# A diffusion block's input projection, done in two sweeps with high and low parts of its weight

## The reference

```python
cq, ckv, kr, rq, rk, rv, rg = jnp.split(h @ w_in, IN_SPLITS, axis=-1)   # widths 256,128,32,512,512,512,512
q_a, k_a, v_a = mla_qkv(cq, ckv, kr, ...)                 # latent attention: norm, w_uq, w_ukv, rope
o_att = block_attention(q_a, [k_a, k_ac], [v_a, v_ac])
q_r, k_r, v_r = retention_qkv(rq, rk, rv, row, col)       # rope; 8 heads of 64
# per chunk of 128 tokens, forwards and backwards in time:
s = einsum(qc, kc) * decay_in;  y_inner = einsum(s, vc);  y_cross = einsum(qc * xi, r_prev)
r = decay_chunk * r + einsum(kc * zeta, vc)               # the carried state
y_ret = norm(y_fwd + y_bwd) * g_ret * silu(rg)
x = x + ga1 * (concat([o_att, y_ret]) @ w_o)              # then the expert layer
```

## Time and profile before

| | us |
|---|---|
| median of 3 runs (lowest, highest) | 3234.02 (3233.12, 3239.76) |
| the profiled execution, its own time | 3241.32 |
| span of its trace, first to last instruction | 3239.5 |
| first product with `w_in` starts | 145.5 |
| last record of the projection starts (L525) | 889.5 |
| retention: first instruction, last one | 897.8, 1103.6 |
| first product of the attention | 1120.0 |

### The profile page before, as it was taken

How to read it: one execution, slowest core, us unless ns; L and a number is a source line. 1 busy time by engine, 2 the same in 40 slices (tenths; PEclk the granted TensorE clock), 3 DMA queues, 4 the chain that set the end, 5 groups by cost and what they waited for, 6 DMA issues and landing times. The chain is left out here.

```text
span 3239.5 us, 55402 instructions
## 1 busy us (share of the span) xinstructions
PE 2990.5 (92%) x20325; PEld 2205.0 (68%) x20325; DVE 2014.4 (62%) x2973; ACT 1381.0 (43%) x2069; POOL 353.2 (11%) x385
## 2 busy tenths in 40 slices
PE   6799999999978699999999998899399999999997
PEld 1355555555578667666666665787398989899996
DVE  1133333333357599989899998445766666666766
ACT  0133333333222377677677765211244444444444
POOL 0011111111145200000000000221001111010102
PEclk9899999999977699999999999999599999999998
DMA  8511111111132301110111000533467676666768
GB/s 313 176 65 64 64 60 61 61 64 64 52 111 78 82 3 34 37 25 14 35 27 25 23 6 12 179 135 113 137 205 209 206 222 208 201 203 211 212 202 312
DMA packets 255042, 365.51 MB, mean 113 GB/s; under 512 B 36469, under 2 KB 170616, under 8 KB 253177
## 3 DMA queue, kind: packets, MB, share of 16 engines
q1 hardware_dynamic: 245336, 327.97, 31.5%
q0 software_dynamic: 9504, 34.61, 4.5%
HBM read 280.70 MB, written 81.83 MB: 112 GB/s over the span
## 5 line engine op out<-in xcount | busy, mean ns | idle before, releaser
L479 PE MATMUL bank<-w_in_sb,h_T 128*128 128x512 f32 (+1 forms) x1440 | 609.9, 578 | 2.1 <-DVE h_T L628 2.1
L1784 PE MATMUL ebank<-gathered_T,w_gate_up 128*128 128x256 f32 x4608 | 561.2, 284 | 21.8 <-issue 16.4
L1784 PEld LDWEIGHTS ebank<-gathered_T,w_gate_up 128*128 128x128 f32 x4608 | 556.7, 193 | 25.6 <-issue 20.7
L479 PEld LDWEIGHTS bank<-w_in_sb,h_T 128*128 128x128 f32 x1440 | 270.4, 191 | 299.4 <-issue 299.1
L1062 PE MATMUL abank<-head_qT,head_kT 96*128 96x512 f32 x1728 | 414.7, 400 | 23.2 <-DVE head_qT L1171 17.0
L1062 PEld LDWEIGHTS abank<-head_qT,head_kT 96*128 96x128 f32 x1728 | 326.3, 192 | 104.6 <-issue 29.6
L1142 ACT ACTIVATE scores<-scores 128x1536 f32<-128x1536 f32 x192 | 274.3, 1476 | 232.8 <-DVE scores L1201 232.8
L1201 DVE TENSOR_TENSOR scores<-scores,abank 128x1536 f32<-128x1536 f32 x192 | 322.7, 1748 | 44.9 <-PE abank L1082 44.8
L1137 ACT ACTIVATE scores<-abank 128x512 f32<-128x512 f32 x576 | 325.7, 602 | 42.5 <-PE abank L1062 17.1
L1092 PE MATMUL abank<-scores,head_v 128*64 128x256 f32 x2304 | 291.0, 388 | 1.2 <-ACT scores L1142 1.2
L1798 PE MATMUL ebank<-w_down,hidden_T 128*128 128x512 f32 x1152 | 282.0, 400 | 2.9 <-DVE w_down L2016 2.8
(11 more groups left out here) (266 smaller groups left out, 3291.8 us busy)
## 6 DMA issues: line engine op xcount, KB each, us to landing
w_gate_up_whole<-in_w_exp_gate SPq DMA_DIRECT2D x48, 1024.0 KB, 5.7
w_gate_up_whole<-in_w_exp_up SPq DMA_DIRECT2D x48, 1024.0 KB, 9.0
w_down_whole<-in_w_exp_down SPq DMA_DIRECT2D x192, 256.0 KB, 6.0
ada_w<-in_w_ada SPq DMA_DIRECT2D x12, 2048.0 KB
scratch_ret<-ret_rows SPq DMA_DIRECT2D x72, 256.0 KB, 2.5
x_tile<-in_x_all SPq DMA_DIRECT2D x18, 512.0 KB
w_in_sb<-in_w_in SPq DMA_DIRECT2D x4, 2048.0 KB, 18.2
chunk_qk<-scratch_ret SPq DMA_DIRECT2D x16, 512.0 KB
```

The lines of the kernel that those rows point to most:

```text
L479: m = pe.matmul(banks[bank][:, 0:n], hT[u][:, k, :], w_in[:, k, lo:lo + n], start=(k == 0), stop=(k == KD - 1))
L1784: x = pe.matmul(banks[f % 3][:, j * CAP:(j + 1) * CAP], w_gu[c][:, wp, j, k, o:o + P], xsT[:, xp, k, :], start=(k == 0 and n == 0), stop=( ...
```

## The change

`w_in` and h are split into high and low parts, and each product is three `fp32r` matmuls. The columns are divided over two sweeps.

**Going up** (`project`, 18 turns): latents, retention keys and values only, 24 matmuls each. h is written to memory (`scratch_h`, 512 KB a tile) before its low part overwrites it, and the chunk's state goes to memory too. Attention queries are made for the 16 latent tiles only. The three weight parts needed here are split during `modulation`, on ACT and DVE. The query and gate columns (4 MB) are loaded at the start of `project` and only used in the next stage.

**Going down** (`retention`, 16 turns): h, keys, values and states are read back; each turn forms the queries and gates of the next chunk (`z_query`, `z_gate`, 24 matmuls each), ropes the query, takes the gate, and does the retention of its own chunk, in this order on each engine. Query and gate weights are split at its start, 16 pieces of 128x512. The scaled-query and score tiles have one buffer instead of two, and scores no longer run ahead.

The core of the diff:

```diff
+
+def modulation(nc, ins, perm, scratch, weights, w_loaded, w_rest):
 
     with stage_semaphores(nc) as sem, ExitStack() as ctx:
...
+            for part, c in enumerate(IN_PARTS):
+                act.wait_ge(w_loaded[1 + part], 16)
+                act.activation(weights["in"][:, 0, :, c], weights["in_whole"][:, 1, :, c], ACT.Copy).then_inc(s_w_in, 1)
...
+                if 5 <= n < 8:
+                    c = IN_PARTS[n - 5]
+                    dve.wait_ge(s_w_in, n - 4)
+                    dve.tensor_tensor(weights["in"][:, 1, :, c], weights["in_whole"][:, 1, :, c], weights["in"][:, 0, :, c].bitcast(F32), ALU.subtract).then_inc(w_rest, 1)
...
+            w_in_cols = ins["w_in"][0].rearrange("(k p) n -> p k n", p=P)
+            for j, c in enumerate((LAT, LAT + 3 * RW)):
+                sp.dma_start(w_qg[:, :, j * RW:(j + 1) * RW], w_in_cols[:, :, c:c + RW]).then_inc(qg_loaded, 16)
+            store(0, "hT", hT_whole[0][:, 1, :, :], scratch["h"][0:P], "h_stored")
...
-                for ready, src, dst, stored in stores:
-                    sg[ready].wait(sp, t)
-                    settled(sp)
-                    sp.dma_start(dst(bass.ds(row, P)), src).then_inc(sg[stored].sem, 16)
...
+                store(t, "ret_k", rk[:, :], scratch["rk"][at, :], "rk_stored")
+                if ahead:
+                    store(t + 1, "hT", hT_whole[1 - u][:, 1, :, :], scratch["h"][bass.ds(row + P, P)], "h_stored")
+                store(t, "latT", krT[:, :], scratch["kT"][4, 0:ROPE, at], "kr_stored")
...
-            def z(u, bank, lo, n):
+            def z(t, u, bank, lo, n):
                 for k in range(KD):
-                    m = pe.matmul(banks[bank][:, 0:n], hT[u][:, k, :], w_in[:, k, lo:lo + n],
-                                  start=(k == 0), stop=(k == KD - 1))
+                    for i, (hp, wp) in enumerate(((0, 0), (0, 1), (1, 0))):
+                        m = pe.matmul(banks[bank][:, 0:n], hT[u][:, hp, k, :], w_in[:, wp, k, lo:lo + n],
+                                      start=(k == 0 and i == 0), stop=(k == KD - 1 and i == 2))
                 m.then_inc(sg["z_psum"].sem, 1)
...
-            def turn(t, u, ahead):
-                sg["hT"].wait(pe, t)
-                sg["ret_v"].wait(pe, t - 1)
-                z(u, 0, 0, LAT)
-                sg["qT_rows"].wait(pe, t - 1)
-                z(u, 1, LAT, RW)
+            def turn(t, u, ahead, queries):
+                sg["h_rest"].wait(pe, t)
+                sg["z_latent"].wait(pe, t - 1)
+                z(t, u, 0, 0, LAT)
+                sg["ret_k"].wait(pe, t - 1)
+                z(t, u, 1, LAT, RW)
+                if ahead:
+                    xT(pe, t + 1, 1 - u)
                 sg["kr_lat"].wait(pe, t)
...
-                sg["gate"].wait(pe, t - 1)
-                z(u, 3, LAT + RW, RW)
+                sg["ret_v"].wait(pe, t - 1)
+                z(t, u, 3, LAT + RW, RW)
                 sg["latT"].wait(pe, t)
+                sg["u_back"].wait(pe, t - 1)
...
+                if queries:
+                    sg["q_roped"].wait(pe, t - TC)
+                    sg["v_rows"].wait(pe, t)
+                    for g in range(2):
+                        for h in range(4):
+                            m = pe.transpose(banks[5 + 2 * g][0:DQ, h * P:(h + 1) * P], q_sb[:, 4 * g + h, :], perm["ident"][:, :])
+                        m.then_inc(sg["qT_psum"].sem, 1)
...
             xT(pe, 0, 0)
-            pe.wait_ge(w_loaded[0], 16 * 6)
+            pe.wait_ge(w_loaded[0], 16 * 3)
+            pe.wait_ge(w_rest, 3)
             loop(pe, turn)
...
+            def round_h(t, u):
+
+                sg["z_psum"].wait(act, t - 2)
+                for g in range(2):
+                    k = slice(4 * g, 4 * g + 4)
+                    sg["hT"].wait(act, t, 2 * g + 2)
+                    act.activation(hT[u][:, 0, k, :], hT_whole[u][:, 1, k, :], ACT.Copy).then_inc(sg["h_rounded"].sem, 1)
+
+            def turn(t, u, ahead, queries):
+                if ahead:
+                    x_stats(t + 1, 1 - u)
...
                 if ahead:
-                    x_stats(t + 1, 1 - u)
...
+                    round_h(t + 1, 1 - u)
+                sg["z_psum"].wait(act, t, 3)
...
+            def rest(t, u):
+
+                sg["h_stored"].wait(dve, t)
+                for g in range(2):
+                    k = slice(4 * g, 4 * g + 4)
+                    sg["h_rounded"].wait(dve, t, g + 1)
+                    dve.tensor_tensor(hT[u][:, 1, k, :], hT_whole[u][:, 1, k, :], hT[u][:, 0, k, :].bitcast(F32), ALU.subtract).then_inc(sg["h_rest"].sem, 1)
...
-                dve.tensor_tensor(rows4[:, row, :], rterm[:, 0, :], rterm[:, 1, :], ALU.add).then_inc(sig.sem, 1)
...
+            def turn(t, u, ahead, queries):
+
+                if ahead:
+                    x_norm(t + 1, 1 - u)
+                if not (isinstance(t, int) and t == 0):
+                    advance_state(t - 1, 1 - u)
...
+                sg["k_zeta"].wait(dve, t - 1)
+                rope_ret(t, u, 1, rk[:, :], RK_SCALE, sg["ret_k"], sg["rk_stored"])
+                if ahead:
+                    modulate(t + 1, 1 - u)
...
-                g = rows4[:, 3, :]
-                sg["gate_exp"].wait(dve, t)
-                dve.tensor_scalar(g, g, 1.0, None, ALU.add).then_inc(sg["gate"].sem, 1)
-                sg["gate"].wait(dve, t, 1)
-                dve.reciprocal(g, g).then_inc(sg["gate"].sem, 1)
-                sg["gate"].wait(dve, t, 2)
-                dve.tensor_tensor(g, banks[3][:, :], g, ALU.mult).then_inc(sg["gate"].sem, 1)
...
+                if ahead:
+                    rest(t + 1, 1 - u)
+
+            dve.memset(st[0][0:64, :], 0.0).then_inc(zero_state, 1)
+            dve.wait_ge(zero_state, 1)
             x_norm(0, 0)
             modulate(0, 0)
+            rest(0, 0)
...
+            def load_h(row, u):
+                sp.dma_start(hT_whole[u][:, 1, :, :], scratch["h"][bass.ds(row, P)]).then_inc(h_loaded.sems[u], 32)
+                sp.dma_start(rope[:, u, :], ins["rope_tables"][bass.ds(row, P), :]).then_inc(h_loaded.sems[u], 32)
...
+                row = (T - 3) * P - r * P
+                if ahead == 2:
+                    sg["z_psum"].wait(sp, r)
+                    settled(sp)
+                    sg["ret_q"].wait(sp, r)
+                    settled(sp)
+                    load_h(row, u)
...
+            def z(r, u, bank, part, first):
+                for k in range(KD):
+                    if first:
+                        pe.wait_ge(w_rest, part * KD + k + 1)
+                    for i, (hp, wp) in enumerate(((0, w_hi), (0, w_lo), (1, w_hi))):
+                        m = pe.matmul(banks[bank][:, :], hT[u][:, hp, k, :], wp[:, k, part * RW:(part + 1) * RW],
+                                      start=(k == 0 and i == 0), stop=(k == KD - 1 and i == 2))
+                m.then_inc(sg["z_psum"].sem, 1)
...
             def turn(r, u, first, ahead):
-                if ahead >= 1:
-                    scores(r + 1)
-                outputs(r, u)
-                if ahead >= 2:
-                    transposes(r + 2, u)
+                if ahead:
+                    z_query(r + 1, 1 - u)
+                scores(r)
                 if not first:
                     out_transposes(r - 1)
-
+                if ahead:
+                    z_gate(r + 1, 1 - u)
+                outputs(r, u)
+                if ahead:
+                    transposes(r + 1, 1 - u)
+
+            z_query(0, 0, True)
+            z_gate(0, 0, True)
             transposes(0, 0)
...
+            def round_h(r, u):
...
+                act.activation(hT[u][:, 0, :, :], hT_whole[u][:, 1, :, :], ACT.Copy).then_inc(sg["h_rounded"].sem, 1)
...
+            def gate_exp(r):
...
+            def turn(r, u, first, ahead):
+                evacuate_kq(r)
+                if not first:
+                    square(r - 1)
+                evacuate_qx(r)
                 if not first:
                     store(r - 1)
-
-            for r in range(2):
-                evacuate_kq(r)
-                evacuate_qx(r, r)
+                if ahead == 2:
+                    round_h(r + 2, u)
+                if ahead:
+                    gate_exp(r + 1)
+
+            round_h(0, 0)
+            for part in range(2):
+                c = slice(part * RW, (part + 1) * RW)
+                for k in range(KD):
+                    act.activation(w_hi[:, k, c], w_whole[:, k, c], ACT.Copy).then_inc(w_rounded, 1)
+            round_h(1, 1)
+            gate_exp(0)
...
+            def split(part):
+                c = slice(part * RW, (part + 1) * RW)
+                for k in range(KD):
+                    dve.wait_ge(w_rounded, part * KD + k + 1)
+                    dve.tensor_tensor(w_lo[:, k, c], w_whole[:, k, c], w_hi[:, k, c].bitcast(F32), ALU.subtract).then_inc(w_rest, 1)
+
+            def rest_h(r, u):
+                sg["h_rounded"].wait(dve, r)
```

(37 more changed lines are left out.)

470 lines of the change are left out of this document (262 added, 208 removed).

## The result

The changed kernel takes 3051 us (median of four runs, 3039 to 3061), where the kernel before takes 3236 (four runs, 3233 to 3240): the ratio of the two is 0.943, 95% interval 0.939 to 0.946. That is 185 us less; the prediction said 161 (3073 us, range 3035 to 3130). Runs of the changed kernel lie further apart than those of the kernel before. The profiled execution took 3061.1 us, with a span of 3059.3, and is the longest of the four, so it stands 10 us above the median.

The account below looks back on a forecast made before the run. The projection was taken as bound by PE's own work, the retention by waits between engines and the half clock. Going up -280 us and down +118 gave -161 (unrounded terms), so 3073 us, range 3035 to 3130.

Parts of the forecast that it names:

- One product: Both sweeps: a 512-column product in high and low parts takes 5.55 us against 6.86 in float32, ratio 0.81.
- PE's work of a turn going up: Projection sweep: products, attention q, k and v, transpositions and state sum to 24.0 us a turn.
- The stall going up: Projection sweep: ACT and DVE let attention q start only at 18.6 us; turn 25.8, 1.8 above PE's work.
- `rest` waits for the store of h: Going up: DVE's low part waits for h's store, ending near 22.5 us, 3 before PE wants it.
- Going down, a turn: Retention sweep: PE's work of 18.6 us sets the turn; DVE's 17.3 fits with 1 us to spare.
- Start and end of the way down: Retention sweep: turn 0 starts at 26 us; after the last outputs 8 us remain; stage sum 324 us.
- Later stages "as long as now": Attention and the stages after it: claimed to keep their present lengths.
- DVE as the bound going down: Retention sweep: SBUF contention with POOL makes turns 22.2 us, 54 us more in all, 3127 us; chance 0.10.
- the half clock there: Going down: clock at 0.72 adds 108 us, giving 3181; chance 0.08 for all or part of the sweep.
- a retention without room: Going down: waits stay 12.9 us and products add 11.1, turns 24.0 us, total 3154 us; chance 0.04.
- The case lower than 3035: Both sweeps: turns reach their floors and there is no contention, total under 3035 us; chance 0.04.
- The slower case: Both sweeps: clock falls to 0.72, adding 165 us up and 108 down, total 3346 us; chance 0.03.

Follow-up runs that it names:

- e2_f32: Changed kernel with the products of both sweeps in float32 and the low parts not computed: 3147.1 us, ratio 0.972 to the kernel before.
- e11_copy: Changed kernel run again unchanged, for a third profile: 3050.3 us.
- e9_best: Changed kernel with five edits against small losses (store order, first product's terms, x statistics, k-zeta, weight rounding): 3032.1 us, ratio 0.935 to the kernel before.
- e7_kzeta_late: Changed kernel with POOL's k-zeta waiting until the next chunk's h is whole, going up: 3040.1 us (one run).
- e5_up_one: Changed kernel with only the high-by-high term of the products computed going up: 3040.3 us (one run).
- e8_store_twice: Changed kernel with each h stored twice going up, low parts waiting for the second store: 3056.0 us (one run).
- e4_down_one: Changed kernel with only the high-by-high term of the query and gate products computed going down: 3032.7 us (one run).
- e6_recip: Changed kernel with DVE computing the gate's reciprocal twice in each turn going down: 3091.5 us (one run).

## Why the prediction was right, and where it was off

The direction, and both mechanisms, held: e2_f32 shows the new division of the work and the shorter products apart, worth 98 and 102 us. The prediction speaks of two gains. Its sum holds a third, the work left out for the two context tiles, some 34 of the 98 us by the estimate above. The forecast for the profiled execution was 3080 us, and it took 3061. The 19 us are two errors of opposite sign: the changed stages came out 34 us shorter than forecast, the others 14.6 longer. That they cancel in part is luck: in e11_copy, the same program, the others are 2.4 us longer than in the first profile of before, and the run took 3050. Without the luck the time is still inside the range.

- **One product.** 5.55 us forecast; 24 matmuls at 0.231, as the row of the output projection had it. Right, and with it the ratio of 0.81 to a float32 product. The prediction's other figure, an estimate of 0.75 from the four passes that the Trainium skill, FP8 and Floating Point Precision, TensorE Precision Notes, counts for true FP32, is not what the rows show.
- **PE's work of a turn going up.** 24.0 us forecast; e9_best, whose turns have no wait, has 23.82.
- **The stall going up: the step that failed.** The forecast walked the chain to 18.6 us at attention q and so had the turn 1.8 above PE's work; it is at 17.3 to 17.45, and the turn of 24.4 is 0.6 above the 23.82. The profile books only part of this as PE's wait: 0.23 us at attention q in 7 of the turns. The walk was right to 0.1 us as far as the latents' copy (5.24 against 5.3) and close to the normed latents (10.96 against 11.2). Too large were the contention with POOL, 1.0 against the 0.34 us of one addition (e7_kzeta_late: 0.4 a turn), and single pieces added end to end, which in the rows start 0.1 us before the last one ends. Sixteen turns at 24.4 instead of 25.8 are 22 of the 28 us by which the way up was shorter (431.5 against 460); the two context turns and the half clock at the start make up the rest. The term was mis-sized, not misplaced: e5_up_one shows that the chain with PE's work behind it is 24.3 to 24.4 us long, and that it, not PE's work, is the bound, as the prediction had it.
- **`rest` waits for the store of h.** Off the path in each turn with queries (done 3.8 us early, 3 forecast); near it in the two context turns, which the prediction did not look at for this wait (e8_store_twice); in the first turn it is the 8.0 us of the waits above. First product at 150.4 (151.7 forecast).
- **Going down, a turn.** PE 18.6 forecast, 18.50 measured; DVE 17.3 and 17.37 (e4_down_one); the product's end as the start of the gate, and 1 us to spare: 1.07. Here the sum of pieces and waits was right. `y_out` takes 0.69 us now, where the earlier trace rows had 1.33; the carried state (L1078) still meets POOL's scaled query and takes 1.45 us, where the same shape in L1071 takes 0.69. The forecast's 1.4 to 2.1 for the two took that in, and the added contention stood only in a rival.
- **Start and end of the way down.** Turn 0 starts 27.5 us after the last work of the way up (32.5 forecast): the sixteen pieces of weights follow each other at 0.61 us, not 0.72. The end is some 2 us longer. Sum 326 for 330.
- **Later stages "as long as now".** The step that failed on the other side. Of the 14.6 us 5.5 are the output projection's, which repeat in each run of the program and whose cause is open; 1.1 lie in the search, and the others in attention and experts, which in profiles of the same program differ by as much (914.0 to 919.0 and 909.3 to 915.4).

Of the rivals, DVE as the bound going down is out (18.50, not 22.2), and so are the half clock there (1.00 from 640 to 885 us, with twenty transpositions in each turn beside the dense products, so what the Trainium skill, TensorE: Matmul & The Clock Gate, Part 4, says of transpositions did not decide) and a retention without room (24.0 a turn). The row of 926 to 934 us, which the prediction took to agree with that page, does not show it: what ran there at the half clock were outputs up to 930.9 and transpositions only behind. The case lower than 3035 needed both floors; the way up came within 0.4 us a turn of the floor of 24.0, and e9_best went below it. The slower case did not come, but its mechanism is real: e5_up_one takes work away from PE and loses 23 us to it.

## What to carry to other kernels

Where two chains are nearly equal, here 24.4 and 23.8 us, taking work from the shorter gains nothing, and can cost: compare the chain of the other engines with PE's work before shortening either, to a few tenths of a microsecond, and look for the bound in a run that leaves one of them out. The profile booked 1.6 us of waits for a difference of some 9 us over 16 turns. Before counting a gain as overlap, take out the work that the new version no longer does. A change of order that puts matmuls beside a stage full of waits pays twice, once for the hidden waits and once for the clock that dense matmuls keep up. Price contention from the very instructions that meet, and leave room in a forecast for the stages that are not touched: over the profiles of this study they lay between 2117 and 2134 us, but for e5_up_one, whose experts had other rows.

## What the hardware showed that was not expected

PE's granted clock differed where the instructions and the waits were the same. In e6_recip one turn was granted 1.00 and the next 0.93, and from 638 to 854 us every third turn was of the second kind. In e4_down_one and e5_up_one, where PE is busy for 81% and 64 to 79% of a stretch, the clock is 0.81 and 0.66 to 0.86. At the start of the way down the same stream of matmuls ran at 1.2 GHz for about 3 us in one program and 6 in another.

ACT stands up to 6.9 us at one place of a stage without anything in the profile that it waits for, the same within 0.1 us in one program (6.80 to 6.89 in three profiles) and another in the next (4.7 in e4_down_one).
